# Hybrid trunk, layer 0 mixers: the first pair's columns prepared earlier, the gate multiply moved behind the forward states

## What is computed

```
u = h @ ssd_w_in
z, xbc, dt_raw, bg, cg, xin = split(u)
xbc = silu(dwconv(xbc, conv_w) + conv_b)
xs, bm, cm = split(xbc)
y_f, s_f = ssd_scan(xs, dt[:, :, 0], a[0], bm, cm, h0[:, 0])
y_b, s_b = ssd_scan(flip(xs), flip(dt[:, :, 1]), a[1], flip(bm), flip(cm), h0[:, 1])
y = y_f + flip(y_b) + xs * d_skip
y = y * silu(z)
y_b = bg * dwconv(cg * xin, sc_conv_w)
```

## Time and profile before

| | |
|---|---|
| median of 3 runs | 1969.57 us (1967.96 to 1970.12) |
| the profiled execution | 1966.25 us, span 1964.5 us |
| PE busy | 1895.6 us, 96% of the span |
| PE weight loads (beside PE) | 1811.7 us, 92% |
| DVE busy | 1031.8 us, 53% |
| ACT, POOL busy | 671.9 us, 636.3 us |
| chain that ended last | PE 88%, DVE 6%, ACT 2%, issue 2% |

### The profile page before, as it was taken

How to read it: one execution, slowest core, us unless ns; L and a number is a source line. 1 busy time by engine, 2 the same in 40 slices (tenths; PEclk the granted TensorE clock), 3 DMA queues, 4 the chain that set the end, 5 groups by cost and what they waited for, 6 DMA issues and landing times.

```text
span 1964.5 us, 35222 instructions
## 1 busy us (share of the span) xinstructions
PE 1895.6 (96%) x13425; PEld 1811.7 (92%) x13425; DVE 1031.8 (53%) x1987; ACT 671.9 (34%) x1021; POOL 636.3 (32%) x309
## 2 busy tenths in 40 slices
PE   5998999999999999999999999989999999999997
PEld 3997888888899999999999999977899999999997
DVE  5647677777722655313554354557466553035543
ACT  4442222332413434312333422137534333123332
POOL 1222222222232233343334433333132333433342
PEclk8999999999999999999999999999999999999999
DMA  8224444454443222222222432211232222222221
GB/s 321 73 86 144 140 159 141 134 165 149 167 150 101 68 73 75 63 77 84 75 63 61 144 92 78 76 39 34 93 89 65 75 72 65 77 75 75 63 67 74
DMA packets 272884, 192.48 MB, mean 98 GB/s; under 512 B 25370, under 2 KB 259222, under 8 KB 271270
## 3 DMA queue, kind: packets, MB, share of 16 engines
q1 hardware_dynamic: 267638, 182.81, 30.2%
q10 hardware_dynamic: 5168, 8.59, 1.2%
HBM read 181.31 MB, written 10.06 MB: 97 GB/s over the span
## 4 chain that ended last, share of the span: by engine, by line
PE 88%; DVE 6%; ACT 2%; issue 2%; DMA 1%; POOL 1%; SPq 0%; DVEq 0%; ACTq 0%; POOLq 0%
PE ps L607 26%; PE ps L611 25%; PE ps L608 25%; PE ps L679 2%; DVE mbuf L1785 1%; PE ps L1034 1%; PE ps L1014 1%; PE ps L856 1%; PE ps L999 1%; DVE mbuf L1777 1%; DVE act_lo L1595 1%; ACT sp L1386 1%; PE ps L686 0%; DMA x<-x_spill 0%; DVE hin L1802 0%
## 5 line engine op out<-in xcount | busy, mean ns | idle before, releaser
L550 POOL TENSOR_TENSOR w_lo<-raw,w_hi 128x1024 fp32r<-128x1024 f32 x244 | 600.0, 2462 | 1238.2 <-ACT w_hi L1087 1238.2
L607 PE MATMUL ps<-act_hi,w_hi 128*128 128x322 f32 x2752 | 846.6, 314 | 6.8 <-DVE act_lo L1595 2.6
L608 PE MATMUL ps<-act_lo,w_hi 128*128 128x322 f32 x2624 | 801.8, 312 | 0.0
L611 PE MATMUL ps<-act_hi,w_lo 128*128 128x322 f32 x2752 | 634.9, 312 | 0.0
L607 PEld LDWEIGHTS ps<-act_hi,w_hi 128*128 128x128 f32 x2752 | 524.5, 191 | 21.7 <-issue 15.9
L608 PEld LDWEIGHTS ps<-act_lo,w_hi 128*128 128x128 f32 x2624 | 497.6, 190 | 0.0
L611 PEld LDWEIGHTS ps<-act_hi,w_lo 128*128 128x128 f32 x2752 | 465.1, 189 | 0.0
L1087 ACT ACTIVATE w_hi<-raw 128x1024 fp32r<-128x1024 f32 x244 | 256.1, 1051 | 371.8 <-PE ps L611 328.4
L607 PE MATMUL ps<-f_hi,w_hi 128*128 128x322 f32 x704 | 214.2, 311 | 0.0
L608 PE MATMUL ps<-f_lo,w_hi 128*128 128x322 f32 x704 | 213.7, 310 | 0.0
L1885 DVE SCALAR_TENSOR_TENSOR x<-ps,mod,x 128x128 f32 (+1 forms) x144 | 54.4, 433 | 266.3 <-PE ps L611 265.8
(11 more groups left out here) (296 smaller groups left out, 1955.6 us busy)
## 6 DMA issues: line engine op xcount, KB each, us to landing
ada<-in_ada_w SPq DMA_DIRECT2D x40, 1024.0 KB, 5.9
raw<-in_ssd_w_in SPq DMA_DIRECT2D x44, 512.0 KB, 3.8
raw<-in_ffn_w_gate SPq DMA_DIRECT2D x44, 512.0 KB, 3.7
raw<-in_ffn_w_up SPq DMA_DIRECT2D x44, 512.0 KB, 3.7
raw<-in_ffn_w_down SPq DMA_DIRECT2D x32, 384.0 KB, 3.0
raw<-in_na_w_qkv SPq DMA_DIRECT2D x24, 512.0 KB, 3.7
raw<-in_ffn_w_down SPq DMA_DIRECT2D x32, 320.0 KB, 2.8
first<-in_ada_w SPq DMA_DIRECT2D x8, 1024.0 KB, 13.2
```

The lines of the kernel that those rows point to most:

```text
L550: g.tensor_tensor(w_lo[:, s], raw[:, s % RAW], w_hi[:, s], ALU.subtract).then_inc(S["low_split"], 1)
L607: t.matmul(out, hi, chunk_of(src_hi, k0 + k, cols), start=start, stop=False)
L608: t.matmul(out, hi, chunk_of(src_lo, k0 + k, cols), start=False, stop=False)
L611: mm = t.matmul(ps[:, 2 * tset + h, 0:HALF], lo, chunk_of(src_hi, k0 + k, cols), start=False, stop=stop)
```

## The change

`prepare` becomes a function of the whole DVE block. `prepare(0)` is called ahead of the last input tile's `conv_in`, once the first `xs` tile is done (`xin_ready` at 5), and no longer after the last one. In every pair the gate multiply, with its wait for the tanh, moves from ahead of `seg(2)` and `states(0)` to behind them. No instruction is added or dropped; PE, ACT, POOL and SP run the same streams as before.

```diff
+            def prepare(j):
+                if not (isinstance(j, int) and j == 0):
+                    dve.wait_ge(S["ctok_ready"], j)
+                v.tensor_copy(xsj[:], xs[:, bass.ds(j * T, T)])
...
+                v.tensor_copy(pick[:], bass.AP(tensor=mine.tensor, offset=mine.offset, ap=[mine.ap[0], [HEADS, 2], [1, 2]]))
...
+                v.tensor_copy(col[:], pair).then_inc(S["prep_ready"], 1)
             for i in range(2):
...
                 for s in range(4):
+                    if (i, s) == (1, 3):
+                        dve.wait_ge(S["xin_ready"], 5)
+                        prepare(0)
                     conv_in(4 + s, i, s, 4 * i + s, 4 * i + 4 + s, xs[:, bass.ds((4 * i + s) * T, T)])
             dve.wait_ge(S["table_stored"], 16)
             dve.wait_ge(S["xin_ready"], IN_SLOTS)
...
                     decayed(0)
+                    seg(2)
+                    states(0)
                     dve.wait_ge(S["gate_tanh"], j + 1)
                     stt(F(zs[:]), F(zs[:]), 1.0, V(0), ALU.add, ALU.mult).then_inc(S["tile_free0"], 1)
-                    seg(2)
-                    states(0)
                     decayed(1).then_inc(S["m_ready"], 1)
...
-                if g == 0:
-                    prepare(0)
                 loops = C // GROUPS - g
```

More of the change, by code:

```diff
@@ L1711, in group_taken @@
                 dve.wait_ge(S["group_ready"], g + 1)
+            def prepare(j):
+                if not (isinstance(j, int) and j == 0):
+                    dve.wait_ge(S["ctok_ready"], j)
+                v.tensor_copy(xsj[:], xs[:, bass.ds(j * T, T)])
+                mine = unit[:, bass.ds(2 * j, HEADS + 2)]
+                v.tensor_copy(pick[:], bass.AP(tensor=mine.tensor, offset=mine.offset, ap=[mine.ap[0], [HEADS, 2], [1, 2]]))
+                scv = sc[:].rearrange("p n k u -> p (n k u)")[:, bass.ds(2 * j, NC * KINDS * 32 - 14)]
+                pair = bass.AP(tensor=scv.tensor, offset=scv.offset, ap=[scv.ap[0], [32, NC * KINDS], [HEADS, 2], [1, 2]])
+                v.tensor_copy(col[:], pair).then_inc(S["prep_ready"], 1)
             for i in range(2):
@@ L1738, in _ @@
                 tb = TILE_MIX + 4 * j0
[L1739 to L1748, removed]
                 def pair_of_heads(i, more=True):
```

## The result

The changed kernel takes 1956.92 us (median of 6 runs, 1955.69 to 1958.22), the kernel before beside it 1968.76 us (6 runs, 1965.03 to 1970.67): ratio 0.9941, interval 0.9929 to 0.9954, 11.84 us less. Forecast were 11.3 us and 1958.3 us.

The account below looks back on a forecast made before the run. PE, busy 96% of the span, was taken as the bound, with gains only where it waits for DVE. 6.75 us in pair 0 plus 4.55 in seven pairs gave 11.3 off 1969.57: 1958.3 us, range 1954 to 1965.

Parts of the forecast that it names:

- Bound: Whole span: PE busy 96%, so DVE steps matter only where PE waits: pair 0's entry and `hin` in each pair.
- Copies: DVE's gap of 3.69 us ahead of the last tile's L1684: three copies take 3.09 us there and cost nothing.
- Pair 0: Entry and first sections of pair 0: 5.94 us earlier at section 1 plus 0.81 us states wait, 6.75 us gained.
- The new wait for the second `ada` block: PE at pair 0's second `ada` section: block requested at 157.18, landing 6.2 us later, a new wait of 1.24 us.
- The wait on the states in this pair: PE ahead of L832 in pair 0: gone because the `ada` wait lets DVE catch up, 0.81 us gained.
- the ceiling: PE's wait on `hin` in each pair: without any wait PE gains at most 0.70 + 0.11 = 0.81 us.
- The gate: Other seven pairs, gate behind the forward states: 0.65 us gained a pair, 4.55 us in all, ends 3.5 and 5.7.
- refill of 0.11 us: PE's half slot after waiting for the gate: possible extra 0.11 us, making the gain as little as 0.51 us a pair.
- The half clock: Rival, pair 0's new `ada` wait: lower clock returns and costs 2.60 us, giving 1960.9 us; chance 0.15.
- The gate did not cost what the states had cost: Rival, half slot in seven pairs: gate ends as late as 262.45, those pairs gain nothing, about 1963 us; chance 0.08.
- L805 was held by nothing else: Rival, pair 0's entry: something unseen holds L805 or L776 until the old time, gates alone gain 5.2, 1964.4 us; chance 0.05.
- POOL never held up the gate: Rival, each pair's gate: it meets POOL's `w_lo`, ends at 263.9, eight pairs lose 11 us, 1975 us; chance 0.03.

Follow-up runs that it names:

- the last kernel: Changed kernel with the three copies of `prepare(0)` inside the last input tile, between its second tap and the tanh wait: 1958.01 us, ratio 0.9941.

## Why the prediction was right

*Bound.* PE at the two places was the right reading: the gains stand where it had waited, 4.58 us of idle time and 2.60 of slow work behind it at the entry, and 0.70 us in each pair.

*Copies.* Counted at 3.09 us in a gap of 3.69; they took 2.89, ending 0.89 us ahead of the last tile. They cost nothing, as forecast, and `pick` did meet POOL's `w_lo` again: the two end 0.02 us apart, and away from `w_lo`, in the last kernel, it took 0.17 us.

*Pair 0.* The opening came as forecast: full clock, 5.44 us to the second `rows_of`. The new wait for the second `ada` block was forecast at 1.24 us and came at 0.98. Against the mark the request left after 6.45 us instead of 6.64 and the block landed after 6.0 us instead of 6.2; L805 started 0.16 us earlier, which by itself lengthens the wait. The gain at section 1, which the block alone sets, was 6.29 us instead of 5.94. The wait on the states in this pair fell away with 0.96 us against the 0.81 that I called the ceiling: L832 behind `rows_of(3)` starts after 0.23 us when nothing holds it, so the idle time in brackets, counted from the modelled end of the matmul before, understated what a wait costs. Pair 0 gave 7.25 us against 6.75. One of its terms was partly luck: the 2.60 us of slow work were taken from a single execution, and the kernel with the gate alone, behind the same 4.6 us of idle time, shows 1.56.

*The gate.* Forecast 0.65 us a pair, measured 0.69, with PE waiting exactly where I had put it: L832 0.05 us behind the states, the half slot 0.06 us behind the gate. There was no refill of 0.11 us on top. A little of the wait on the states stayed, 0.13 us (L832 0.36 us behind `rows_of(3)` instead of 0.23), too short for the brackets; the forecast had it below 0.1. Seven pairs gave 4.73 against 4.55. That the sum of the parts meets the medians within 0.7 us is closer than their interval can confirm.

*Rivals.* The half clock did not come back in pair 0: in the five traces with an `ada` wait there of 0.98 to 1.25 us, L679 behind it took 1.06 or 1.07 us, its full-clock length. The rule that I had weighed from the Trainium skill, page "TensorE: Matmul & The Clock Gate", section "HAM oscillation — how this bites in real kernels", thus cost nothing here; behind a longer wait it showed in half of the traces, as the last section tells. The case on that page is a loop that waits for data at every tile; it does not say that a single short wait must bring the half rate, and my prediction read it too widely. The gate did not cost what the states had cost, though PE waits for it now, and the kernel with the later gate shows that every further delay of it comes out of PE. L805 was held by nothing else. POOL never held up the gate: all eight took 0.82 us.

## What to carry to other kernels

Once a wait on a chain of two results is shortened, look at the next thing that the waiting engine needs: here the half slot needed the gate, and the gain ended where the gate ended. An operation between a result and its waiter can be moved behind the result, but only as far as its own waiter allows; one step more turned a gain of 0.6% into a loss of 0.4%. When a start is pulled forward, follow the in-order queue that feeds it: its requests may be tied to another engine's pace and become the new wait.

## What the runs showed that I had not expected

The price of one and the same idle time varies with the clock. At the change of head groups PE idles 2.85 or 2.86 us ahead of L805 in all ten traces, but the stretch from there to the second `rows_of` takes 5.46 us in five and 6.81 to 7.04 us in the other five. The changed kernel and the one with the `ada` block ahead:

```profile
328.15 0.63 PE L805 MATMUL ps<-ident,xsj 128*128 128x128 f32 x4 [2.85 <-DVE btok L1710]
...
335.14 0.40 PE L776 MATMUL ps<-sum_rows,pick 128*128 128x256 f32 x2
```

```profile
326.85 0.63 PE L805 MATMUL ps<-ident,xsj 128*128 128x128 f32 x4 [2.85 <-DVE btok L1710]
...
332.31 0.39 PE L776 MATMUL ps<-sum_rows,pick 128*128 128x256 f32 x2
```

6.99 us in the first, where the granted clock behind it fell to the lower level, and 5.46 in the second, where it stayed at 1.00:

```profile
330.00:332.00 2.00, 2.00 (x10) 1.74 (x7) 1.94 (x6) 0.03 (x1) 0.00 (x0) 0.50 0.34 47
```

```profile
330.00:332.00 2.00, 2.00 (x15) 2.00 (x14) 0.64 (x3) 0.63 (x1) 0.00 (x0) 1.00 0.92 262
```

At the entry to pair 0, the same 4.6 us of idle time cost 2.60 us of slow work in the kernel before and 1.56 in the kernel with the gate alone (7.00 us from L805 to the second `rows_of`). In the kernel with the later gate the waits of 2.05 to 2.14 us were followed by the low clock in two pairs out of seven, at 1.56 and 1.57 us, within one execution. In these traces a wait thus has a fixed price, its length, and a variable one of 0 to some 2.6 us. Runs of one kernel differ by 2 to 7 us, and a few such prices would make up that much, though the single runs were not taken apart to show it. What a trace shows at the place of the change is therefore a surer measure than the spans of two traces. What decides in a given execution whether the clock falls was not tried.
